# Dense gate and up products: one 512-column matmul over high and low tokens side by side, the halves added outside TensorE

## The reference, cut to what matters

```
def swiglu(t, w_gu, w_down):
    g, u = jnp.split(t @ w_gu, 2, axis=-1)
    return (jax.nn.silu(g) * u) @ w_down
```

## Time and profile before

| | |
|---|---|
| median of 3 runs | 1276.79 us (1276.14 to 1277.42) |
| the profiled execution's own time | 1277.29 us |
| its span, first to last instruction | 1275.4 us |
| busy TensorE (matmuls) | 1251.6 us, 98% |
| busy VectorE / ScalarE / GpSimd | 386.9 / 214.3 / 109.7 us |
| mean granted TensorE clock | 0.997 |
| dense SwiGLU on TensorE | from 67.97 us to about 259 us of the span |

### The profile page before, as it was taken

How to read it: one execution, slowest core, us unless ns; L and a number is a source line. 1 busy time by engine, 2 the same in 40 slices (tenths; PEclk the granted TensorE clock), 3 DMA queues, 4 the chain that set the end, 5 groups by cost and what they waited for, 6 DMA issues and landing times.

```text
span 1275.4 us, 31402 instructions
## 1 busy us (share of the span) xinstructions
PE 1251.6 (98%) x14693; PEld 783.4 (61%) x14693; DVE 386.9 (30%) x591; ACT 214.3 (17%) x320; POOL 109.7 (9%) x134
## 2 busy tenths in 40 slices
PE   7999999999999999999999999999999999999997
PEld 4699999889774354545555454554545545454555
DVE  1567778878882110101101011010101201011012
ACT  3254343474741000000000000000000000000001
POOL 4220000010030000020020010002001000200100
PEclk9999999999999999999999999999999999999999
DMA  9998999959279999999999999999999999999980
GB/s 371 414 380 295 337 337 307 357 203 395 102 265 420 424 423 424 423 406 424 424 406 423 424 408 412 424 411 402 423 421 396 423 424 408 405 424 419 398 356 36
DMA packets 114056, 477.49 MB, mean 374 GB/s; under 512 B 10944, under 2 KB 37280, under 8 KB 113792
## 3 DMA queue, kind: packets, MB, share of 16 engines
q1 hardware_dynamic: 106112, 457.29, 89.3%
q0 software_dynamic: 7664, 17.87, 4.5%
q10 hardware_dynamic: 144, 0.26, 0.1%
HBM read 465.79 MB, written 11.16 MB: 374 GB/s over the span
## 4 chain that ended last, share of the span: by engine, by line
PE 95%; DVE 2%; ACT 1%; POOL 1%; DMA 1%; issue 0%; SPq 0%; DVEq 0%; ACTq 0%
PE ps L2427 23%; PE ps L2413 23%; PE ps L2402 23%; PE ps L1927 7%; PE ps L1928 7%; PE ps L1929 7%; PE ps L1952 1%; PE ps L2014 1%; PE ps L1911 1%; DMA raw<-w_mod 1%; DVE wlo L1572 1%; PE ps L2214 1%; PE ps L1975 0%; PE ps L2356 0%; PE ps L1999 0%
## 5 line engine op out<-in xcount | busy, mean ns | idle before, releaser
L1799 DVE TENSOR_TENSOR act_in<-act_in,ps 128x1344 f32<-128x1344 f32 x16 | 24.9, 1554 | 527.2 <-PE ps L2413 527.2
L1927 PE MATMUL ps<-thi,whi 128*128 128x256 f32 x480 | 136.0, 283 | 0.7 <-DVE wlo L1421 0.7
L1928 PE MATMUL ps<-tlo,whi 128*128 128x256 f32 x480 | 135.8, 283 | 0.0
L1929 PE MATMUL ps<-thi,wlo 128*128 128x256 f32 x480 | 135.8, 283 | 0.0
L2402 PE MATMUL ps<-raw,turned_in 128*32 128x448 f32 x1296 | 123.7, 539 | 0.0
L2413 PE MATMUL ps<-ring_w,turned_in 128*32 128x448 f32 x1248 | 120.6, 539 | 0.0
L2427 PE MATMUL ps<-ring_w,turned_act 128*32 128x256 f32 x2016 | 117.2, 379 | 0.0
L2427 PE MATMUL ps<-raw,turned_act 128*32 128x256 f32 x2016 | 115.5, 379 | 0.0
L1220 ACT ACTIVATE act_in<-ps 128x1344 f32<-128x1344 f32 x16 | 20.7, 1291 | 548.6 <-PE ps L2402 548.6
L2427 PEld LDWEIGHTS ps<-raw,turned_act 128*32 128x32 f32 x2016 | 82.5, 110 | 33.4 <-issue 3.5
L1290 DVE TENSOR_TENSOR wlo<-raw,whi 128x2048 fp32r<-128x2048 f32 x41 | 92.9, 2288 | 32.8 <-ACT whi L901 32.8
(11 more groups left out here) (324 smaller groups left out, 1337.3 us busy)
## 6 DMA issues: line engine op xcount, KB each, us to landing
raw<-moe_w_gu SPq DMA_DIRECT2D x96, 896.0 KB, 13.3
ring_w<-moe_w_gu SPq DMA_DIRECT2D x96, 896.0 KB, 12.9
raw<-w_mod SPq DMA_DIRECT2D x84, 512.0 KB, 5.7
rows<-moe_w_gu SPq DMA_DIRECT2D x48, 896.0 KB
raw<-moe_w_down SPq DMA_DIRECT2D x48, 896.0 KB, 14.3
ring_w<-moe_w_down SPq DMA_DIRECT2D x48, 896.0 KB, 13.8
raw<-ffn_w_gu SPq DMA_DIRECT2D x44, 512.0 KB, 5.5
rows<-moe_w_down SPq DMA_DIRECT2D x24, 896.0 KB
```

Of the source, the lines that this page charges most:

```text
L1799: dve.tensor_tensor(act_3, act_3, gate_up_ps(1), ALU.mult).then_inc(e_act, 1)
L1927: pe.matmul(out, a_hi, b_hi, start=start, stop=False, skip_group_check=check)
L1928: pe.matmul(out, a_hi, b_lo, start=False, stop=False, skip_group_check=check)
L1929: return pe.matmul(out, a_lo, b_hi, start=False, stop=stop, skip_group_check=check)
```

## The change

In the dense gate and up products, `thi` and `tlo` become one tensor `turned`, in which the 256 high and the 256 low tokens of an input block lie side by side. One matmul 512 wide multiplies the high weights with both; a second, 256 wide, adds the low weights by the high tokens to the first half. Each of the four products of a chunk takes a PSUM bank of its own, `2 * g + jj`, so all four banks 0 to 3 are used by every chunk. ScalarE copies the second halves of the four banks to SBUF (`ffn_cross`), VectorE adds the first halves to them (`ffn_sum`), and silu and the product with the up part then work in SBUF. The next chunk's `ffn_gate_up` waits for `f_sum`. Other edits: of the modulation units of a step only the first (`ahead`) stays before the down unit, the others move behind it, in the loads and in VectorE's order; `row_sum(0, 5)` moves behind the down products of chunk 9 for the first tile and waits for `f_sum`; the two loads into `wide_src` share a semaphore, and TensorE waits for both at once.

```diff
+def ahead(mods):
+
+    return min(len(mods), 1)
...
-        thi = sb("thi", [P, UNIT], F32R)
-        tlo = sb("tlo", [P, UNIT], F32R)
+        turned = sb("turned", [P, KC, 2, S], F32R)
...
+        thi3, tlo3 = turned[:, :, 0, :], turned[:, :, 1, :]
+        turned_pair = turned[:, :, :, :].rearrange("p k t s -> p k (t s)")
...
-        last_hi, last_lo = thi[:, 0:512], tlo[:, 0:512]
+        last_hi, last_lo = turned_pair[:, 0, :], turned_pair[:, 1, :]
...
-            pool.dma_start(wide_src[:, 0:D], pool_scale[0:1, :]).then_inc(scale_loaded, 16)
-            pool.dma_start(wide_src[:, D:2 * D], norm_g[0, 1:2, :]).then_inc(first_gain_loaded, 16)
+            pool.dma_start(wide_src[:, 0:D], pool_scale[0:1, :]).then_inc(wide_loaded, 16)
+            pool.dma_start(wide_src[:, D:2 * D], norm_g[0, 1:2, :]).then_inc(wide_loaded, 16)
...
+            def ffn_cross(s):
+
+                act.wait_ge(unit_used, 3 * s + 1 if s else 2)
+                if s:
+                    act.wait_ge(f_alo, s)
+                act.copy(tmp[:, 0:1024].rearrange("p (g s) -> p g s", g=4), ps[:, 0:4, S:2 * S]).then_inc(f_sg, 1)
+
             def ffn_act(s):
 
+                act.wait_ge(f_sum, s + 1)
+                act.activation(sg, sg, ACT.Silu).then_inc(f_sg, 1)
+                act.wait_ge(f_act, s + 1)
                 act.wait_ge(unit_used, 3 * s + 2)
-                b = 2 * (s % 2)
-                act.activation(sg.rearrange("p (j s) -> p j s", j=2), ps[:, b:b + 2, 0:FC], ACT.Silu).then_inc(f_sg, 1)
-                act.wait_ge(f_act, s + 1)
                 act.activation(ahi[:, :], actf, ACT.Copy).then_inc(f_ahi, 1)
 
             for s, r, q, mods, _ in FFN_STEPS:
                 high(r, q)
+                ffn_cross(s)
                 high(r + 1, q + 1)
                 ffn_act(s)
-                high(r + 2 + len(mods), q + 2)
+                high(r + 2 + ahead(mods), q + 2)
             high(R_LAST_DOWN, Q_LAST_DOWN)
...
+            def ffn_sum(s):
+
+                both = tmp[:, 0:1024].rearrange("p (g s) -> p g s", g=4)
+                dve.wait_ge(f_sg, 2 * s + 1)
+                dve.tensor_tensor(both, ps[:, 0:4, 0:S], both, ALU.add).then_inc(f_sum, 1)
+
             def ffn_act(s):
...
+                dve.wait_ge(f_sg, 2 * s + 2)
+                dve.tensor_tensor(actf, sg, actf, ALU.mult).then_inc(f_act, 1)
...
             for s, r, q, mods, n in FFN_STEPS:
                 low(r, q)
+                ffn_sum(s)
                 low(r + 1, q + 1)
                 if s == 4:
                     lambda_products()
-
-                m = min(len(mods), 2)
+                ffn_act(s)
+                m = ahead(mods)
                 gemv_units(r + 2, mods[:m], n)
-                ffn_act(s)
-                gemv_units(r + 2 + m, mods[m:], n + m)
                 ffn_low(s, alo[:, :], ahi[:, :])
-                low(r + 2 + len(mods), q + 2)
+                low(r + 2 + m, q + 2)
+                gemv_units(r + 3 + m, mods[m:], n + m)
             low(R_LAST_DOWN, Q_LAST_DOWN)
-            dve.wait_ge(f_alo, NCF - 1)
+            ffn_sum(NCF - 1)
             ffn_act(NCF - 1)
...
             def ffn_gate_up(s, r, q, first=False):
 
+                if s:
+                    pe.wait_ge(f_sum, s)
...
-                                o = ps[:, 2 * (s % 2) + jj, g * S:g * S + S]
-                                mm = three(o, whi[:, sl, c0:c0 + P], wlo[:, sl, c0:c0 + P], thi3[:, k, :], tlo3[:, k, :],
-                                           k == 0 and g == 0, k == KC - 1 and g == 1, True)
+                                pe.matmul(bank(2 * g + jj), whi[:, sl, c0:c0 + P], turned_pair[:, k, :],
+                                          start=(k == 0), stop=False, skip_group_check=True)
+                                mm = pe.matmul(ps[:, 2 * g + jj, 0:S], wlo[:, sl, c0:c0 + P], thi3[:, k, :],
+                                               start=False, stop=(k == KC - 1), skip_group_check=True)
...
-            pe.wait_ge(f_alo, NCF - 1)
-            row_sum(0, 5)
...
+            pe.wait_ge(f_alo, NCF - 1)
             down_tile(0, ahi, alo, (q + 2) % SPL, False)
+            pe.wait_ge(f_sum, NCF)
+            row_sum(0, 5)
             pe.wait_ge(f_alo, NCF)
```

More of the change, by code:

```diff
@@ L423, in build_trunk @@
         wr_loaded = sem("wr_loaded")
-        scale_loaded = sem("scale_loaded")
+        wide_loaded = sem("wide_loaded")
         gain_loaded = [sem(f"gain_loaded{i}") for i in range(2)]
         bmod_loaded = [sem(f"bmod_loaded{i}") for i in range(4)]
-        first_gain_loaded = sem("first_gain_loaded")
         wide_ps = sem("wide_ps")
@@ L480, in build_trunk @@
         mix_ps = sem("mix_ps")
+        f_sum = sem("f_sum")
         f_sg = sem("f_sg")
@@ L621, in _ @@
                 load(r + 1, 0, gu_unit(w_gu, FF, s + 1, 1))
-                for i, mod in enumerate(mods):
+                m = ahead(mods)
+                for i, mod in enumerate(mods[:m]):
                     load(r + 2 + i, 0, mod_unit(*mod))
-                load(r + 2 + len(mods), 0, down_unit(w_dn, s))
+                load(r + 2 + m, 0, down_unit(w_dn, s))
+                for i, mod in enumerate(mods[m:]):
+                    load(r + 3 + m + i, 0, mod_unit(*mod))
             load(R_LAST_DOWN, 0, down_unit(w_dn, NCF - 1))
@@ L983, in high_shifted @@
                 act.wait_ge(col_ready, 4)
-                act.activation(thi[:, k * S:k * S + S], hv[:, k * S:k * S + S], ACT.Identity, bias=modc[:, 3, k:k + 1]).then_inc(ht_hi, 1)
+                act.activation(thi3[:, k, :], hv[:, k * S:k * S + S], ACT.Identity, bias=modc[:, 3, k:k + 1]).then_inc(ht_hi, 1)
             for k in range(KC):
@@ L999, in _ @@
                 high(r, q)
+                ffn_cross(s)
                 high(r + 1, q + 1)
                 ffn_act(s)
-                high(r + 2 + len(mods), q + 2)
+                high(r + 2 + ahead(mods), q + 2)
             high(R_LAST_DOWN, Q_LAST_DOWN)
-            act.wait_ge(unit_used, 3 * NCF - 2)
-            b = 2 * ((NCF - 1) % 2)
-            act.activation(sg.rearrange("p (j s) -> p j s", j=2), ps[:, b:b + 2, 0:FC], ACT.Silu).then_inc(f_sg, 1)
+            ffn_cross(NCF - 1)
+            act.wait_ge(f_sum, NCF)
+            act.activation(sg, sg, ACT.Silu).then_inc(f_sg, 1)
             act.wait_ge(f_act, NCF)
@@ L1133, in turned_heads @@
                 act.wait_ge(ot_ps, b + 1)
-                act.activation(thi[:, 512 * b:512 * b + 512], turned_bank(b), ACT.Copy, scale=subln[:, 1:2]).then_inc(ot_hi, 1)
+                act.activation(thi3[:, 2 * b:2 * b + 2, :], turned_bank(b).rearrange("p (k s) -> p k s", k=2), ACT.Copy, scale=subln[:, 1:2]).then_inc(ot_hi, 1)
             turned_heads(0)
@@ L1427, in low_shifted @@
                 dve.wait_ge(ht_hi, k + 1)
-                dve.scalar_tensor_tensor(tlo[:, part], hv[:, part], modc[:, 3, k:k + 1], thi[:, part].bitcast(F32),
+                dve.scalar_tensor_tensor(tlo3[:, k, :], hv[:, part], modc[:, 3, k:k + 1], thi3[:, k, :].bitcast(F32),
                                          ALU.add, ALU.subtract).then_inc(ht_lo, 1)
@@ L1652, in turned_low @@
                 dve.wait_ge(ot_hi, b + 1)
-                dve.scalar_tensor_tensor(tlo[:, 512 * b:512 * b + 512], turned_bank(b), subln[:, 1:2],
-                                         thi[:, 512 * b:512 * b + 512].bitcast(F32), ALU.mult, ALU.subtract).then_inc(ot_lo, 1)
+                dve.scalar_tensor_tensor(tlo3[:, 2 * b:2 * b + 2, :], turned_bank(b).rearrange("p (k s) -> p k s", k=2), subln[:, 1:2],
+                                         thi3[:, 2 * b:2 * b + 2, :].bitcast(F32), ALU.mult, ALU.subtract).then_inc(ot_lo, 1)
             head_square(NH - 3)
@@ L1976, in spread @@
                 mm.then_inc(wide_ps, 1)
-            pe.wait_ge(scale_loaded, 16)
+            pe.wait_ge(wide_loaded, 32)
             spread(0, 2)
@@ L2099, in _ @@
                 ffn_gate_up(s + 1, r, q)
-                ffn_down(s, r + 2 + len(mods), q + 2)
+                ffn_down(s, r + 2 + ahead(mods), q + 2)
             _, r, q, mods, _ = FFN_STEPS[-1]
             ffn_gate_up(NCF - 1, r, q)
-            pe.wait_ge(f_alo, NCF - 1)
-            row_sum(0, 5)
             def down_tile(t, hi_part, lo_part, sl, last):
@@ L2118, in down_tile @@
                 return mm
-            pe.wait_ge(unit_done, finished(r + 2 + len(mods)))
+            pe.wait_ge(unit_done, finished(r + 2 + ahead(mods)))
+            pe.wait_ge(f_alo, NCF - 1)
             down_tile(0, ahi, alo, (q + 2) % SPL, False)
+            pe.wait_ge(f_sum, NCF)
+            row_sum(0, 5)
             pe.wait_ge(f_alo, NCF)
```

8 lines of the change are left out of this document (1 added, 7 removed).

## The result

The changed kernel takes 1278.65 us (median of 20 runs, 1277.71 to 1279.53), the kernel before 1276.96 us in its 20 runs. The ratio is 1.0014, with a 95% interval of 1.0008 to 1.0020: slower by 1.7 us. That is within the 0.2% that I called no change and inside the stated range. But the sum had come out at -0.6 us: it missed by 2.3 us, and its sign was wrong.

The account below looks back on a forecast made before the run. TensorE was taken to bound the dense part: -4.26 us from fewer matmuls, +1.63 from a stall at the start and +2.07 from one at the end gave -0.56 us, a median of 1276.2 us. Range: 1272.5 to 1279.6 us.

Parts of the forecast that it names:

- the sum: Whole kernel: -4.26 from matmuls, +1.63 and +2.07 from two stalls, -0.56 us in all, median 1276.2 us.
- What bounds the kernel: Dense part: TensorE sets the pace, busy all 16.98 us of a chunk; gains or losses there move everything behind.
- The copy and the sum in the chunks: Chunks 1 to 9: ScalarE copy 1.015 us, VectorE sum 1.220 us, hidden behind a 5.46 us down stage.
- The stall at the start: Ahead of chunk 1: no down stage covers chunk 0's copy and sum, so TensorE loses 1.63 us.
- The stall at the end: Behind the last gate-up products: TensorE waits for VectorE's late sum and the work after it, losing 2.07 us.
- the backlog's share: End of the dense part: VectorE's late work makes the loss 2.07 us, where without backlog it would be 0.8.
- The matmuls: Gate-up products: a 512 and a 256 take 0.3476 us where three 256s took 0.3597, saving 4.26 us.
- A: Rival, gate-up matmuls: weight load fits easily after a 512, pair 0.3344 us, saving 8.9, total 1271.6 us; chance 0.18.
- B: Rival, gate-up matmuls: extra belongs to columns, pair 0.36 us, stalls stay, 1280.5 us; chance 0.12 with longer stalls.
- C: Rival, end of dense part: no backlog forms, stall 0.8, 1274.9 us; counted within the forecast's 0.70.
- the 2.5 ns: Skill page's extra per matmul: 352 left out would save 0.9 us, giving 1279.6; forecast used the trace's 13 to 14 ns.

Follow-up runs that it names:

- widths in sixteens: Changed kernel with 16 gate-up matmuls of 512 columns, then 16 of 256, per unit from chunk 1 on: 1276.92 us, 1.0003 of the kernel before.
- Run 1: Changed kernel with only the 512-column gate-up matmul cut again into two of 256: 1279.84 us, 1.0027 of the kernel before.
- runs 5 to 7: Changed kernel, gate-up matmuls reordered: four 512s then four 256s; eight in a row to one bank; both: 1277.69, 1278.30, 1277.70 us.
- run 8: Changed kernel without any 256-column gate and up matmul (low weights with high tokens), so work is left out: 1256.29 us, one run.
- run 9: The kernel with widths in sixteens: changed kernel, 16 matmuls of 512 then 16 of 256 per unit from chunk 1 on: 1276.92 us, ratio 1.0003.
- in fours: Changed kernel with four gate-up matmuls of 512 columns, then four of 256, per input block: 1277.69 us, 1.0005 of the kernel before.

## Why the prediction was right and where it was wrong

**What bounds the kernel: right.** TensorE sets the pace of the dense part, and what the part loses goes through to the end: 1.78 us there, 1.7 us in the median.

**The copy and the sum in the chunks: right.** The copy takes 1.016 us and the sum 1.224 us, by groups of the changed kernel, against 1.015 and 1.220 taken from the earlier trace rows; in chunks 1 to 9 no wait shows.

```profile
L1475 DVE TENSOR_TENSOR tmp<-ps,tmp 128x1024 f32<-128x1024 f32 x11 | 13.5, 1224 | 16.6 <-ACT tmp L1002 16.6
L1002 ACT COPY tmp<-ps 128x1024 f32<-128x1024 f32 x11 | 11.2, 1016 | 40.0 <-PE ps L2099 40.0
```

**The stall at the start: right.** 1.64 us, 1.63 forecast, and a free set of banks ends it.

**The stall at the end: right in size, in part by luck.** The last down products start 6.64 us behind the last gate-up start, 251.23 - 244.59, where it was 249.35 - 244.76 = 4.59: 2.05 us (2.07 forecast). The mechanism was tested: an even load on VectorE shortens this stall by 1.2 us, and I had put the backlog's share at 2.07 - 0.8 = 1.27. But 2.07 was worked out for chunks of 16.59 us. The kernel with widths in sixteens has such chunks, and there the stall is 7.07 - 4.59 = 2.48 us:

```profile
240.68 1.28 DVE L1317 SCALAR_TENSOR_TENSOR rows<-raw,silu_c,rows 128x1024 f32<-128x1024 f32 x1 [0.46 <-DVE rows L1319]
245.40 1.22 DVE L1475 TENSOR_TENSOR tmp<-ps,tmp 128x1024 f32<-128x1024 f32 x1
249.45 0.50 PE L1947 MATMUL ps<-whi,turned 128*128 128x512 f32 x1 [0.79 <-DVE turned L1309]
```

The first line shows a piece that the sum lacked. VectorE pauses for 0.46 us ahead of the last modulation unit, where it pauses for about 0.1 us between others. Every kernel with the change has this pause, the changed one too; the kernel before doesn't:

```profile
242.46 1.29 DVE L1317 SCALAR_TENSOR_TENSOR rows<-raw,silu_c,rows 128x1024 f32<-128x1024 f32 x1 [0.46 <-DVE rows L1319]
```

Its cause is open: the row names only VectorE's own unit before it, and the chain that ended last calls 0.40 us of it "issue", time in which the engine waits for nothing that the profile shows. In the changed kernel the pause was made up for by two chunks that were each 0.2 us longer than forecast: the last sum starts 2.59 us behind the last gate-up start there (247.18 - 244.59), in sixteens 3.02 (245.40 - 242.38).

**The matmuls: wrong, and this is the step that failed.** It reads: "I take the sum of the two measured steps, since all 94 and all 22 go at one rhythm". The pair cost 0.3532 us in place of 0.3476. So the pairs saved 352 x (0.3597 - 0.3532) = 2.3 us and not 4.26, and the whole of the gate-up part saved 2.1 (table below). Run 1 showed the pair's worth from the other side, runs 5 to 7 that the turns cost something and the change of bank nothing, run 8 that the wide matmul alone keeps the step of the down products, and run 9 that with sixteens the forecast price is reached.

The sentence had a second fault, which the trace of the kernel before shows. The 22 don't go at one rhythm. The down products of chunk 0 follow on 256-column matmuls, and their first steps are longer than the later ones (timeline of TensorE):

```profile
91.94 0.28 PE L1929 MATMUL ps<-thi,wlo 128*128 128x256 f32 x1
92.06 0.40 PE L1927 MATMUL ps<-whi,ahi 128*128 128x512 f32 x1
92.29 0.40 PE L1928 MATMUL ps<-wlo,ahi 128*128 128x512 f32 x1
92.53 0.39 PE L1929 MATMUL ps<-whi,alo 128*128 128x512 f32 x1
...
93.90 0.39 PE L1929 MATMUL ps<-whi,alo 128*128 128x512 f32 x1
94.12 0.39 PE L1927 MATMUL ps<-whi,ahi 128*128 128x512 f32 x1
```

Over the eight down stages between 90 and 228 us, the first five steps are 0.228 to 0.236 us, 0.232 in the mean, and all others 0.227. The mean of 0.2277 hid that. In strict turns every wide matmul stands just behind a narrow one, and there it takes 0.236 us.

**The whole dense part.** By the starts on TensorE, in us:

| | before | changed | in sixteens |
|---|---|---|---|
| first to last gate-up start of chunk 0 | 11.50 | 11.29 | 11.21 |
| to the first of chunk 1 | 1.00 | 2.64 | 2.64 |
| to the last gate-up start of chunk 10 | 164.29 | 162.42 | 160.32 |
| to the first down product of chunk 10 | 4.59 | 6.64 | 7.07 |
| to the turned tile | 11.70 | 11.87 | 11.83 |
| dense part | 193.08 | 194.86 | 193.07 |

The first and third rows are the gate-up products with the down stages between them: they saved 2.08 us in the changed kernel and 4.26 in sixteens, where 4.26 was forecast. So the changed kernel's sum is -2.08 + 1.64 + 2.05 + 0.17 = +1.78 us. The 0.17 stood in no term of the forecast; some 0.1 of it is the longer first step behind the last wait, 0.34 us from 251.23. In sixteens it is -4.26 + 1.64 + 2.48 + 0.13 = -0.01 us: even at the forecast price of a pair the change wins nothing, since the two ends take back all of it.

**The rivals.** A was to decide under a pair of 0.342 us and B over one of 0.3565; 0.3532 lies between forecast and B, nearer to B, whose sign came true. A's reason plays little part: the 256-column matmul behind a wide one takes 0.117 us in the mean where it took 0.120, and A had asked for 0.1067. B's reason, that the extra belongs to the columns, is not what the runs show: with the widths in sixteens the saving is all there. C did not come true: the backlog formed. As for the Trainium skill's page TensorE: Matmul & The Clock Gate, Back-to-back issue gap, the 2.5 ns above the columns that it gives for the isolated step was too small here in every order: in sixteens the extra is 0.2269 - 0.2133 = 13.6 ns for 512 columns and 0.1194 - 0.1067 = 12.7 ns for 256.

## What to carry to other kernels

Before adding up steps of matmuls from a trace, look whether the new stream keeps them between the same neighbours, and look at single steps and not only at their mean: here 512 and 256 columns in turns gave back half of what the wider matmul saved, and a reordering without any other edit brought it back. A change that makes an engine's work in a steady loop cheaper but takes away its double buffering can be paid for at the two ends of the loop, as here, where no other stage covers the new chain; count those ends first, and look for a buffer that is idle only then (banks 4 to 7 ahead of the first down stage). An engine that is busy for 96% of a chunk (VectorE's 16.12 of 16.79 us) may cause no wait in the loop and still deliver its backlog at the loop's end. And where a term comes out right, check that it does so under the conditions it was worked out for: the stall at the end did so only because the chunks were longer than forecast.

## What the runs showed of the hardware that was not expected

Two matmuls, one of 512 and one of 256 columns, each with new weights, take 0.353 us together when they alternate. In turns of sixteen they take 0.346 us, and writing to the same or to another PSUM bank made no difference (16.79 us per chunk either way). The chunk took 16.79 us with turns of one, 16.69 with turns of four and 16.57 with turns of sixteen. So the cost is not a fixed price per change of width: 24 fewer returns per chunk saved 0.11 us and the next 6 fewer as much again. The steps by their place in a row of one width show where it goes (means from the traces, between 100 and 228 us, granted clock 1.00):

| kernel, row | steps in order, us |
|---|---|
| in turns of one | 512: 0.236; 256: 0.117 |
| in fours, gate-up | 512: 0.233, 0.234, 0.231, 0.229; 256: 0.117, 0.119, 0.119, 0.118 |
| in sixteens, gate-up | 512: 0.230, 0.231, 0.228, 0.230, 0.229, then 0.227; 256: 0.113, 0.119, then 0.120 |

Behind narrow matmuls some five wide ones in a row take up to 0.01 us more than the 0.227 they settle at. In turns of one and of four all of them are among these first; in sixteens eleven of sixteen are not. The down products of the kernel before show it too, with five longer steps. In the changed kernel the first ten steps of a down stage take 0.233 us in the mean, and the stage takes 0.04 us more. Narrow neighbours are not the only thing that brings it on: in run 8, which has none, the nine steps that follow the first one behind the wait at 132.63 take 0.231 us in the mean, and the later ones 0.227. What inside TensorE causes this was not found out.
